# Two norms of a two-block transformer kernel take their mean in two steps; twelve chunks of a weight stream stand elsewhere

## What is computed

```python
u = a * sigmoid(g)
u = conv_general_dilated(u, dw, padding=((30, 0),), feature_group_count=d) + dw_b
u = silu(layer_norm(u, ln_g, ln_b))            # mu, then mean((u - mu)^2)
return u @ w_out + b_out
...
out = mixer_a(h, ...)                          # second block, layer 0
x = layer_norm_2(alpha * x + gate * out, ln_g[i], ln_b[i])
ctx = layer_norm_2(alpha * ctx + gate_c * out_c, ln_g[i], ln_b[i])
h = x * (1 + scale) + shift                    # layer 1: its q, z, k, v units follow
```

## Time and profile before

| | us |
|---|---|
| median of 3 runs | 1242.81 (1241.67 to 1252.16) |
| the profiled execution, its own time | 1244.79 |
| its span, first to last instruction | 1243.0 |
| granted TensorE clock, mean over the span | 0.986 of full speed |
| HBM read, over the span | 226.60 MB, 183 GB/s |

### The profile page before, as it was taken

The page is one execution under the profiler, slowest core; times in us unless marked ns, Lnnn a source line. Parts: engine busy times, 40 slices in busy tenths (PEclk is TensorE's granted clock), DMA queues, the critical chain, the costliest instruction groups (busy, mean ns, idle before and its releaser), DMA issues.

```text
span 1243.0 us, 18770 instructions
## 1 busy us (share of the span) xinstructions
PE 1181.0 (95%) x7782; PEld 1028.6 (83%) x7782; DVE 904.7 (73%) x1344; ACT 561.8 (45%) x743; POOL 51.2 (4%) x69
## 2 busy tenths in 40 slices
PE   2898999999999999999999999999999999999897
PEld 1786798888898878889999888888888888888677
DVE  6866578888878776698887775676767673677666
ACT  2422566665554465574455422323212331564773
POOL 0000000000000021000000000000000000000650
PEclk8899999999999999999999999999999999999998
DMA  9698258787759632567665444333343243232000
GB/s 382 229 325 303 81 195 327 286 308 301 264 211 337 241 133 102 217 234 286 246 247 194 158 182 150 122 134 126 138 177 136 102 157 139 68 136 102 1 2 34
DMA packets 37780, 233.51 MB, mean 188 GB/s; under 512 B 4656, under 2 KB 9008, under 8 KB 10432
## 3 DMA queue, kind: packets, MB, share of 16 engines
q1 hardware_dynamic: 35136, 229.99, 50.5%
q10 hardware_dynamic: 2560, 2.33, 0.7%
HBM read 226.60 MB, written 1.05 MB: 183 GB/s over the span
## 4 chain that ended last, share of the span: by engine, by line
PE 84%; DVE 7%; ACT 4%; DMA 2%; issue 2%; POOL 1%; SPq 0%; ACTq 0%; DVEq 0%
PE prod L1689 18%; PE prod L1690 18%; PE prod L1691 18%; PE prod L1695 11%; PE prod L1696 5%; PE misc L1677 2%; DMA raw<-stream 2%; DVE w_lo L988 2%; PE misc L1605 2%; ACT w_hi L583 1%; PE misc L1838 1%; PE misc L1940 1%; POOL cond L972 1%; PE misc L1650 1%; PE prod L1917 1%
## 5 line engine op out<-in xcount | busy, mean ns | idle before, releaser
L988 DVE TENSOR_TENSOR w_lo<-raw,w_hi 128x2048 fp32r<-128x2048 f32 x135 | 309.2, 2291 | 231.7 <-ACT w_hi L583 231.4
L583 ACT ACTIVATE w_hi<-raw 128x2048 fp32r<-128x2048 f32 x135 | 258.4, 1915 | 428.5 <-PE prod L1691 298.0
L1689 PE MATMUL prod<-X_both,w_hi 128*128 128x256 f32 (+1 forms) x912 | 292.6, 321 | 8.9 <-DVE w_lo L988 6.1
L1690 PE MATMUL prod<-X_both,w_hi 128*128 128x256 f32 (+1 forms) x912 | 287.6, 315 | 0.0
L1691 PE MATMUL prod<-X_both,w_lo 128*128 128x256 f32 (+1 forms) x912 | 287.6, 315 | 0.0
L1689 PEld LDWEIGHTS prod<-X_both,w_hi 128*128 128x128 f32 x912 | 174.3, 191 | 24.5 <-DVE w_lo L988 7.1
L1690 PEld LDWEIGHTS prod<-X_both,w_hi 128*128 128x128 f32 x912 | 174.5, 191 | 11.1 <-issue 0.7
L1691 PEld LDWEIGHTS prod<-X_both,w_lo 128*128 128x128 f32 x912 | 174.3, 191 | 10.7
L1695 PE MATMUL prod<-X_both,w_hi 128*128 128x512 f32 x400 | 143.2, 402 | 1.6 <-DVE X_both L1179 0.9
L1689 PE MATMUL prod<-F_both,w_hi 128*128 128x256 f32 (+1 forms) x448 | 140.9, 314 | 0.0
L1691 PE MATMUL prod<-F_both,w_lo 128*128 128x256 f32 (+1 forms) x448 | 140.4, 313 | 0.0
(11 more groups left out here) (277 smaller groups left out, 1714.7 us busy)
## 6 DMA issues: line engine op xcount, KB each, us to landing
raw<-stream SPq DMA_DIRECT2D x210, 1024.0 KB, 4.9
F_both<-V SPq DMA_DIRECT2D x32, 71.0 KB, 2.3
F_both<-V ACTq DMA_DIRECT2D x32, 71.0 KB, 2.6
X<-x_features SPq DMA_DIRECT2D x1, 1024.0 KB, 11.2
V<-cond_rows SPq DMA_DIRECT2D x1, 1024.0 KB, 8.0
C<-ctx_features SPq DMA_DIRECT2D x1, 1024.0 KB, 7.0
out_features<-HT SPq DMA_DIRECT2D x4, 256.0 KB, 2.2
cond<-cond_rows SPq DMA_DIRECT2D x1, 512.0 KB, 4.0
```

The source lines that it names most:

```text
L583: A(halves(w)[0].rearrange("p k c -> p (k c)"), raw[:, n % RING, :], ACT.Copy).then_inc(weight_hi, 1)
L988: ins = tt(lo.rearrange("p k c -> p (k c)"), raw[:, n % RING, :], hi.rearrange("p k c -> p (k c)").bitcast(F32), ALU.subtract)
L1689: mm(out, lhs_hi, rhs_hi, start=start, stop=False)
L1690: mm(out, lhs_hi, rhs_lo, start=False, stop=False)
```

## The change

Norms 1 and 5 join norm 7 in FIRST_MEAN and BY_TOKEN: their mean is taken over the first 4 and 6 tiles, corrected afterwards, and the variance is made in token columns. In norm 1, tiles 4 to 7 are no longer copied out of PSUM by ACT: DVE adds the bias and takes the first mean off in one instruction (`take_conv`), and the last block lies in the bank pair of unit 7. Sigmoid and multiplication become one Silu on ACT. Filler matmuls are 2+6 in place of 16 at unit 8, and 2+3 in place of 8 at MIX_B. The split of unit 9 moves into the joint on DVE, that of MIX_B+1 ahead of it, into the free half of X_both. The sums of the context tiles C (8 matmuls) go behind unit MIX_B. The first twelve chunks after the initial eight stand at units 5, 6 (3), 8 (3), 9 (4), 10 in place of 3 (2), 5, 6, 8 (2), 9 (4), 10, 11.

```diff
@@ -105,8 +105,7 @@
 MOD_BEFORE[0] = 8
 for s in (
-    3, 3, 5, 6, 8, 8, 9, 9,
-    9, 9, 10, 11,
+    5, 6, 6, 6, 8, 8, 8, 9, 9, 9, 9, 10,
     14, 15, 17, 19,
...
-AHEAD = {MLP0 + 1: 1, QKV + 1: 0, MLP1 + 1: 1}
+AHEAD = {MLP0 + 1: 1, QKV + 1: 0, MLP1 + 1: 1, MIX_B + 1: 2}
-LAST = [MLP0 - 1, QKV - 1, MLP1 - 1, NW - 1]
-KEEP_BUSY = {0: 6, CONV_OUT: 16, MLP0: 2, QKV: 2, MLP1: 2, MIX_B: 8}
-FIRST_MEAN = {7: 6}
-BY_TOKEN = (2, 3, 4, 7)
-SPREAD_IN = {MLP0: (2, 3), QKV: (3, 3), MLP1: (4, 3)}
+LAST = [MLP0 - 1, QKV - 1, MLP1 - 1, MIX_B - 1, NW - 1]
+KEEP_BUSY = {0: 6, CONV_OUT: 2, MLP0: 2, QKV: 2, MLP1: 2, MIX_B: 2}
+FIRST_MEAN = {1: 4, 5: 6, 7: 6}
+BY_TOKEN = (1, 2, 3, 4, 5, 7)
+SPREAD_IN = {CONV_OUT: (1, 6), MLP0: (2, 3), QKV: (3, 3), MLP1: (4, 3), MIX_B: (5, 3)}
...
         def conv_bank(j):
-            bank = prod[:, 2, 0:2 * T] if j == 2 else misc[:, min(j, 1), :]
+            if j == 3:
+                return tiles(CONV_OUT - 1, T)
+            bank = prod[:, 2, 0:2 * T] if j == 2 else misc[:, j, :]
             return bank.rearrange("p (i t) -> p i t", i=2)
 
         def halves(w):
             if w in AHEAD:
+                if AHEAD[w] == 2:
+                    return XH[:, :, T:2 * T], XL[:, :, T:2 * T]
...
                 elif n == CONV_OUT:
-                    conv_copy(2)
-                    conv_copy(3)
-                    squares(1, CV, H, lambda k: act.wait_ge(centred, k + 1))
+                    nc.scalar.preload_act_table(ACT.Sqrt)
+                    square_pairs(1, CV, (0, 2, 4))
+                    squares(1, CV, H, lambda k: act.wait_ge(centred, k + 1), (6, 7))
                     rstd(1)
-                    for k in range(KT + 2):
+                    for k in range(KT + 1):
                         if k < KT:
                             act.wait_ge(h_scaled, 8 + k + 1)
-                            A(TS[:, k, :], H[:, k, :], ACT.Sigmoid, bias=cl("conv_ln_b", k))\
-                                .then_inc(silu_sigmoid, 1)
-                        if k >= 2:
-                            act.wait_ge(silu_done, k - 1)
-                            A(XH[:, k - 2, 0:T], TS[:, k - 2, :], ACT.Copy).then_inc(acts_hi, 1)
+                            A(TS[:, k, :], H[:, k, :], ACT.Silu, bias=cl("conv_ln_b", k))\
+                                .then_inc(silu_done, 1)
+                        if k >= 1:
+                            act.wait_ge(silu_done, k)
+                            A(XH[:, k - 1, 0:T], TS[:, k - 1, :], ACT.Copy).then_inc(acts_hi, 1)
...
                 elif n == MIX_B:
-                    squares(5, X, H, lambda k: act.wait_ge(centred, 8 + k + 1))
+                    squares(5, X, H, lambda k: act.wait_ge(x_updated, XU_A + 28 + k - 5), (6, 7))
                     rstd(5)
                     biased_hi(5, 8, lambda k: shift3[:, 0, k:k + 1], H, 0, 56)
+                    A(rows[:, 2, :], rs_row(5), ACT.Copy).then_inc(rs_copied, 1)
...
                 elif n == CONV_OUT:
-                    centre(1, CV)
-                    variance(1, EPS)
-                    dve.wait_ge(rstd_ready, 2)
-                    for k in range(KT + 3):
+                    def take_conv(k):
+                        stt(out=CV[:, k, :], in0=conv_bank(k // 2)[:, k % 2, :], scalar=cl("conv_dw_b", k),
+                            in1=first_mu, op0=ALU.add, op1=ALU.subtract).then_inc(centred, 1)
+                        dve.wait_ge(centred, k + 1)
+
+                    dve.wait_ge(conv_copied, 4)
+                    take_first_mean(1, CV, 4)
+                    dve.wait_ge(conv_summed, 3)
+                    take_conv(4)
+                    take_conv(5)
+                    tt(rest, CV[:, 4, :], CV[:, 5, :], ALU.add).then_inc(rest_added, 1)
+                    split_lo(CONV_OUT + 1)
+                    add_squares(1, (0, 1))
+                    dve.wait_ge(conv_half, 1)
+                    take_conv(6)
...
+                    add_squares(1, (2,))
+                    dve.wait_ge(conv_summed, 4)
+                    take_conv(7)
...
+                    take_rest_mean(1, CV, EPS)
+                    dve.wait_ge(rstd_spread, 1)
+                    for k in range(KT + 2):
                         if k < KT:
                             scale_tile(1, k, CV, H, lambda k: cl("conv_ln_g", k))
-                        if 1 <= k < KT + 1:
-                            i = k - 1
-                            dve.wait_ge(silu_sigmoid, i + 1)
-                            stt(out=TS[:, i, :], in0=H[:, i, :], scalar=cl("conv_ln_b", i),
-                                in1=TS[:, i, :], op0=ALU.add, op1=ALU.mult).then_inc(silu_done, 1)
...
                 elif n == MIX_B:
-                    centre(5, X)
-                    variance(5, LN_EPS)
+                    add_rest(5, X)
+                    take_rest_mean(5, X, LN_EPS)
                     scale_and_split(5, 8, X, H, lambda k: gain3[:, 0, k:k + 1],
                                     lambda k: shift3[:, 0, k:k + 1])
+                    drain(MIX_B - 1, (1,))
...
                 if early:
-                    drain(s - 2)
+                    drain(s - 2, (0,) if s - 1 == MIX_B else (0, 1))
+                if s == MIX_B:
+                    take_first_mean(5, X, KT)
...
@@ -1669,8 +1707,6 @@
                 pe.wait_ge(u_shifted[j % 2], 16 * SHIFTS * SHIFTS * (j // 2 + 1))
-                if j == 3:
-                    pe.wait_ge(conv_copied, 4)
...
+                    if j == 3 and i == 0:
+                        ins.then_inc(conv_half, 1)
...
                     conv(2)
                     conv_sums(1)
                     conv(3)
-                    conv_sums(2)
-                    conv_sums(3)
-                    sum_squares(1, H)
+                    token_columns(1)
...
                 elif n == MIX_B:
-                    for j in (2, 3):
-                        early_sums(5, j)
-                    sum_squares(5, H)
+                    token_columns(5)
...
                 unit(w)
+                if w == MIX_B - 2:
+                    for j in range(3):
+                        early_sums(5, j)
+                if w == MIX_B:
+                    sum_tiles(1, T, C, lambda k: pe.wait_ge(x_updated, XU_A + 32))
```

More of the change, by code:

```diff
@@ L410, in build @@
         recentred = sem("recentred")
+        rs_copied = sem("rs_copied")
+        conv_half = sem("conv_half")
         var_prep = sem("var_prep")
@@ L1523, in _ @@
             for s in range(NW + 2):
-                early = s - 1 == A_OUT_2 or s > 1 and (s - 1 in FIRST_OF_SET or UNITS[s - 2][0] == "conv_g")
+                early = s - 1 == A_OUT_2 or s == MIX_B or s > 1 and (s - 1 in FIRST_OF_SET or UNITS[s - 2][0] == "conv_g")
                 if early:
-                    drain(s - 2)
+                    drain(s - 2, (0,) if s - 1 == MIX_B else (0, 1))
+                if s == MIX_B:
+                    take_first_mean(5, X, KT)
                 if s == WO + 1:
@@ L1538, in _ @@
                         dots(BESIDE[s], (0,))
-                    if s not in AHEAD and s not in BEHIND:
+                    if s not in AHEAD and s not in BEHIND and s != CONV_OUT + 1:
                         split_lo(s)
@@ L1559, in _ @@
                     silu_cond(2, cond[:, :, :], cond_2, cond_t)
+                if s == MIX_B:
+                    add_squares(5, (0, 1))
                 if s == NW:
@@ L1707, in unit @@
                     pe.wait_ge(drained[who], n)
+                if w == MIX_B + 1:
+                    pe.wait_ge(rs_copied, 1)
                 wh, wl = halves(w)
```

41 lines of the change are left out of this document (28 added, 13 removed).

## The result

| | before | after |
|---|---|---|
| median, us | 1242.97 (1237.83 to 1252.16, 8 runs) | 1234.96 (1233.27 to 1238.23, 8 runs) |
| the profiled execution's own time | 1244.79 | 1238.23 |
| its span | 1243.0 | 1236.4 |
| granted clock, mean over the span | 0.986 | 0.979 |

What follows compares the result with a forecast made beforehand. TensorE, busy 95% of the span, bounds the kernel; time is won where it idles or does non-unit work. -5.0 - 3.4 - 0.8 - 3.1 + 1.2 = -11.1 us gives a 1231.8 us median, range 1227.5 to 1237.

Steps and rivals of the forecast that it cites:

- rival D: Ahead of conv(3): unit 8's weights land late, conv(3) 3.7 us later than before, total 1236.3; chance 0.15.
- The chain of norm 1: Joint behind the filter: from conv(3)'s result to the first scaling, 10.0 us becomes 5.0, minus 5.0 us.
- First scaling to the end of unit 8: Joint behind the filter: fewer operations a tile, 8.6 us against 12.0, minus 3.4 us.
- the sign of being wrong that I had named: Joint behind the filter: ACT's pace above 0.8 us a tile would show the forecast wrong.
- Ahead of the filter: Units 3 to 8: PE's 2.87 us wait goes, unit 7's drain starts earlier; minus 0.8 us, ends minus 2.9 and plus 3.7.
- The joint to the query units: Around MIX_B, last mixer unit to query units: 15.8 us removed, 12.7 added, minus 3.1 us.
- The clock: Both joints, with less filler: one fall of TensorE's granted clock in two joints, plus 1.2 us.
- Two of four: Clock falls at existing places: stayed up at 362 and 502 us, fell at 173 and behind norm 7.
- rival B: Granted clock falls in both changed joints, total 1233.1 us; chance 0.15.
- The cover of 3 to 4 us: Before conv(3) ends near 130 us: squares ready near 126, so conv(3) hides them with 3 to 4 us over.
- rival E: Joint behind the filter: unit 9's split, ahead of the squares, delayed by late-landing weights; total 1234.4 us; chance 0.10.
- F: Clock stays at its lower level from conv(3) to the end of unit 8, total 1244.2 us; chance 0.05.

Runs made afterwards that it cites:

- chunks_only: Kernel before with nothing changed but the twelve chunks at their new places; 1242.75 us, ratio 1.0015.
- old_chunks: Changed kernel with the twelve chunks back at their old places, both norms in two steps; 1237.87 us, ratio 0.9964.
- fill_conv3: Changed kernel plus 16 products of 256 columns, result unused, in TensorE's wait ahead of conv(3); 1233.74 us, ratio 0.9932.

## Why the prediction was right, and where it was off

**The result lay in the range** and on the side forecast, and "within 1%" was right. The two joints gave, in the way predicted, 11 of the 11.5 us of their terms. The 3.2 us by which the forecast is missed come from several terms: 0.5 in unit 8, up to 0.8 ahead of the filter, 1.2 more for the clock, and up to 1.5 for a wait that I had put down to a late landing. That the result still falls inside the range is partly luck, for the range's slow end (1237) was drawn for rival D, which did not happen. By its steps:

- **The chain of norm 1, -5.0:** measured 5.07 against 10.0. Right; the end of the program was a fair copy.
- **First scaling to the end of unit 8, -3.4:** 9.1 and not 8.6, so -2.9. Silu cost what Sigmoid had, and its table load (133.03 to 134.31) ended before the first scaled tile. The pace up to the seventh copy is 0.85 us a tile (135.90 to 141.00) where I took 0.79, the sign of being wrong that I had named; but the eighth follows after 0.31, at 141.31, 6.74 us behind the first scaling against 6.8 in my sum. The term that was mis-sized is the last: I had counted six matmuls and 0.3 us behind the last tile, 1.0 us. That tile is ready near 142.2, but PE begins the one before it only at 141.91 and has its last twelve matmuls until 143.6.
- **Ahead of the filter, -0.8:** this step failed. PE's 2.87 us near 60 us do go, in every profile with the new row and in none with the old one, but conv(3)'s end moved from profile to profile far more than by the chunks: 122.0 to 130.0 with the old row (five profiles), 124.7 to 129.4 with the new one (four). The wait turns up again ahead of conv(3), 6 to 8 us in place of 1.4 to 5, as predicted, and behind it conv(3) runs slower, which I had not priced, because the one profile that I had already showed the slow form. Nor does the drain of unit 7 come earlier by what I took: it begins at 105.9 to 107.9 with the new row and at 105.9 to 109.1 with the old one, and the slowest copy then takes 3.9 to 5.5 us with the new row where three of the five profiles with the old one show 3.0 to 3.3. At equal clock chunks_only is 0.5 us under before and old_chunks 0.3 to 0.8 over after: worth 0 to 0.8, not shown.
- **The joint to the query units, -3.1:** -3.07 in most profiles, 1239.44 against 1243.00 alone. Right, with its parts (5.08 for 5.0, 6.9 for 6.8).
- **The clock, +1.2:** right in kind, mis-sized, and looked for in the wrong places. "Two of four" was itself a draw: over fourteen profiles the clock falls at the joints of 362 and 502 in 7 and 8, where my one profile had none. At the two joints of the change, eight profiles with both new norms show no fall in three, one in four, and both (rival B) only in fill_conv3. A fall in the joint at MIX_B costs 0.2 to 0.5 us (three of nine profiles); one in the joint of norm 1 cost after 0.1 us, since it came in filler with slack, and 1.4 to 2.0 us where it came during the column sums. But falls elsewhere (354, 494, 1106, 1154) took 5.5 us from the first profile of after (0.75, 1.6, and 3.1 for the last two). Over the timed runs the mean clock is 0.0025 lower, 2.4 us.
- **The cover of 3 to 4 us, and rival E:** this step failed too. The cover was a product of the one profile: conv(3) ended at 130 there because its last copy landed late (5.5 us) and because it ran 2.8 us slow. In the other four profiles with the old row it ends at 122.0 to 124.9, the cover is gone, and with the new norm 1 DVE then ends last, by 0.9 to 3.1 us. I gave E 0.10 for a late landing of unit 9; it acts in all five profiles with the new norm 1 in which conv(3) ended less than 19 us after the drain and DVE's list had its chunks. It also works as a balance: the faster conv(3) is behind a given drain, the longer the wait, so filler gained nothing.

With these sizes the sum is -5.0 - 2.9 - 3.1 - (0 to 0.8) + 2.4 + (0 to 1.5 for E), -7.1 to -9.4, against -8.0 and -9.0 in the two comparisons. The term for E goes by old_chunks (15.82 against 14.26 us); where the clock fell behind DVE's wait, it was 2.8 to 5 us. Rival D did not come as priced (the drain of unit 7 stood at 107.85 in after, 107.87 before), and F in no profile.

What stays open: why the mean clock is lower in kernels with the new norm 1 (0.980 to 0.985, nine groups, against 0.983 to 0.985 in the others), and what decides a single fall. The Trainium skill (TensorE: Matmul & The Clock Gate, section Why this matters for your kernels) advises against idle gaps between bursts of matmuls. The table agrees: conv(3) took 7.1 us after waits of up to 2.97 us or behind filler, and 8.6 to 9.9 after waits of 5.04 and more. For the falls in the middle of busy stretches (352 to 356: PE busy 4.00 of 4.00) no such gap is there. What PE did just before this one was 24 matmuls of one column (350.41 to 353.15 in after), but the same 24 stand before the same place in profiles without a fall, so my rows give no cause for the single one.

## What to carry over

Before costing a step from one profile, ask which of its durations are draws: a second profile of the unchanged kernel moved the end of the filter by 8 us. Cover counts only if it is there in the fast case; here it was made of a slow clock and a late copy. Count it from the event that starts both sides (here one drain), not from the clock on the wall. And filler in a wait must be shorter than the shortest wait it replaces, or it is the new wait.
